# Where the matmul operands begin in SBUF: shifted starts in the input and activation buffers of a hybrid attention layer

## The reference, cut to what matters

```
p   = rms_norm(x, g_pre) @ w_in                  # 1024 -> 5064 columns: queries, keys, values, indexer, gates
o_a = sliding-window attention;  o_b = indexer, top 256 keys, attention over them
x   = x + rms_norm((sigmoid(g_a) * o_a + sigmoid(g_b) * o_b) @ w_o, g_post_mix)
hid = square(relu(rms_norm(x, g_pre_mlp) @ w_up))            # 1024 -> 4096
y   = x + rms_norm(hid @ w_down, g_post_mlp)                 # 4096 -> 1024
```

## Time and profile before

| | |
|---|---|
| median of 3 runs | 1902.87 us (1902.35 to 1903.76) |
| the profiled execution: its time | 1903.1 us |
| its span of instructions | 1901.3 us |
| TensorE matmul busy | 1879.1 us, 99% |
| TensorE weight load busy | 1778.6 us, 94% |
| VectorE, ScalarE, GpSimd busy | 1136.7, 712.9, 611.2 us |

### The profile page before, as it was taken

How to read it: one execution, slowest core, us unless ns; L and a number is a source line. 1 busy time by engine, 2 the same in 40 slices (tenths; PEclk the granted TensorE clock), 3 DMA queues, 4 the chain that set the end, 5 groups by cost and what they waited for, 6 DMA issues and landing times.

```text
span 1901.3 us, 32833 instructions
## 1 busy us (share of the span) xinstructions
PE 1879.1 (99%) x11892; PEld 1778.6 (94%) x11892; DVE 1136.7 (60%) x2694; ACT 712.9 (37%) x1424; POOL 611.2 (32%) x493
## 2 busy tenths in 40 slices
PE   9999999999999999999999999999999999999997
PEld 8899999877778999999998889999999999999996
DVE  5259999999765667676664553333333333333336
ACT  5345554233345556555673442222222222222222
POOL 4225554134344334444341022222222222222223
PEclk9999999999999999999999999999999999999999
DMA  6433333233556444444323331111111111111114
GB/s 205 116 84 85 99 95 94 83 107 91 124 134 144 102 102 102 102 102 91 68 69 126 114 126 45 45 44 44 44 44 44 44 44 44 44 44 44 44 44 144
DMA packets 180398, 160.26 MB, mean 84 GB/s; under 512 B 101472, under 2 KB 148432, under 8 KB 180288
## 3 DMA queue, kind: packets, MB, share of 16 engines
q1 hardware_dynamic: 164816, 139.72, 25.9%
q10 hardware_dynamic: 15472, 19.09, 4.4%
HBM read 120.63 MB, written 39.27 MB: 84 GB/s over the span
## 4 chain that ended last, share of the span: by engine, by line
PE 93%; DVE 2%; DMA 0%; issue 0%; SPq 0%; ACT 0%; DVEq 0%
PE ps L1084 23%; PE ps L1906 20%; PE ps L2472 19%; PE ps L1806 11%; PE ps L1782 6%; PE ps L1764 5%; PE ps L2153 5%; PE ps L1056 2%; PE ps L2134 0%; PE ps L2000 0%; DVE y L2416 0%; PE ps L1111 0%; DVE probs L1692 0%; DMA m_in<-merged_scr 0%; DVE total L2396 0%
## 5 line engine op out<-in xcount | busy, mean ns | idle before, releaser
L2472 PE MATMUL ps<-hid_hi,weights 128*128 128x362 f32 (+1 forms) x1536 | 380.3, 327 | 0.0
L1906 PE MATMUL ps<-x2T_hi,weights 128*128 128x362 f32 (+1 forms) x1536 | 378.0, 326 | 0.0
L1906 PEld LDWEIGHTS ps<-x2T_hi,weights 128*128 128x128 f32 x1536 | 272.1, 188 | 0.1
L2396 DVE TENSOR_TENSOR total<-total,ps 128x362 f32<-128x362 f32 (+1 forms) x360 | 189.2, 532 | 138.5 <-PE ps L2472 138.5
L2472 PEld LDWEIGHTS ps<-hid_hi,weights 128*128 128x128 f32 x1536 | 270.4, 188 | 0.0
L1906 PE MATMUL ps<-x2T_lo,weights 128*128 128x362 f32 (+1 forms) x768 | 251.4, 327 | 0.0
L2472 PE MATMUL ps<-hid_lo,weights 128*128 128x362 f32 (+1 forms) x768 | 250.2, 326 | 0.0
L1084 PE MATMUL ps<-xT_hi,w 128*128 128x362 f32 (+1 forms) x960 | 246.1, 330 | 1.6 <-PEq L181 1.6
L2381 DVE TENSOR_TENSOR hidden<-hidden 128x362 f32<-128x362 f32 (+1 forms) x96 | 51.5, 537 | 293.5 <-ACT hidden L2356 293.5
L1893 POOL TENSOR_TENSOR weights<-down_raw,weights 128x512 fp32r<-128x512 f32 x64 | 83.8, 1312 | 380.6 <-ACT weights L1887 380.6
L1035 DVE MATCH_REPLACE8 score<-top,score 128x1024 f32<-128x1024 f32 (+5 forms) x208 | 199.3, 967 | 0.0
(11 more groups left out here) (200 smaller groups left out, 3332.8 us busy)
## 6 DMA issues: line engine op xcount, KB each, us to landing
q_raw<-q_scr SPq DMA_DIRECT2D x80, 256.0 KB, 5.0
w_raw<-in_w_in ACTq DMA_DIRECT2D x64, 256.0 KB, 3.0
up_raw<-in_w_up SPq DMA_DIRECT2D x64, 256.0 KB, 2.8
down_raw<-in_w_down SPq DMA_DIRECT2D x64, 256.0 KB, 2.6
gates<-gate_scr SPq DMA_DIRECT2D x34, 256.0 KB, 4.5
x_in<-in_x_prompt SPq DMA_DIRECT2D x16, 512.0 KB, 5.2
gate_scr<-stage SPq DMA_DIRECT2D x32, 256.0 KB, 3.1
q_scr<-stage SPq DMA_DIRECT2D x40, 181.0 KB, 3.1
```

What stands on the lines that cost most here:

```text
L1906: last = pe.matmul(ps[:, bank, 0:n], a[:, k, fs], b, start=(k == 0 and i == 0), stop=(k == KT - 1 and i == 2))
L2396: dve.tensor_tensor(out, out, more, ALU.add).then_inc(added, 1)
L2472: more = pe.matmul(ps[:, falling_bank(g, final), 0:n], a[:, f, cols], h, start=(f == 0 and i == 0), stop=(f == FT - 1 and i == 2))
```

## The change

The three pairs of activation buffers become flat and 32 fp32 elements (128 bytes) longer, and the data begin some elements into them: 10 elements (40 bytes) for `xT` and `x2T`, 2 elements (8 bytes) for `hid`. The helper `moved` returns the same three-dimensional view as before, shifted. The sums by which later tensors are placed grow with it: 256 bytes for each pair. No instruction, wait or transfer is added or removed.

```diff
+def moved(tensor, first, rows, n):
+    return tensor[:, first:first + rows * n].rearrange("p (k n) -> p k n", n=n)
+
+LINE, X_FIRST, HIDDEN_FIRST = 32, 10, 2
-X_BYTES = 2 * 4 * KT * N_TOK
+X_BYTES = 2 * 4 * (KT * N_TOK + LINE)
...
-    out = place(nc, *first, FOOT, ("xT_hi", [P, KT, N_TOK], F32R), ("xT_lo", [P, KT, N_TOK], F32R), ("w", [P, 4, KT, 512], F32R),
+    out = place(nc, *first, FOOT, ("xT_hi", [P, KT * N_TOK + LINE], F32R), ("xT_lo", [P, KT * N_TOK + LINE], F32R), ("w", [P, 4, KT, 512], F32R),
...
-    return out | {"w_lo": out["w"][:, 0:4:2], "w_hi": out["w"][:, 1:4:2]}
+    return out | {"w_lo": out["w"][:, 0:4:2], "w_hi": out["w"][:, 1:4:2]} | \
+        {n: moved(out[n], X_FIRST, KT, N_TOK) for n in ("xT_hi", "xT_lo")}
...
-AFTER_TOTAL = UP_RAW_END + 4 * (2 * D + 2 * 364 + 2 * FT * N_QUERY + KT * N_QUERY)
+AFTER_TOTAL = UP_RAW_END + 4 * (2 * D + 2 * 364 + 2 * (FT * N_QUERY + LINE) + KT * N_QUERY)
...
-        hid_hi = sb("hid_hi", [P, FT, N_QUERY], F32R)
-        hid_lo = sb("hid_lo", [P, FT, N_QUERY], F32R)
+        hid_hi = moved(sb("hid_hi", [P, FT * N_QUERY + LINE], F32R), HIDDEN_FIRST, FT, N_QUERY)
+        hid_lo = moved(sb("hid_lo", [P, FT * N_QUERY + LINE], F32R), HIDDEN_FIRST, FT, N_QUERY)
...
-            x2T = [ctx.enter_context(nc.sbuf_tensor(n, [P, KT, N_QUERY], F32R)) for n in ("x2T_hi", "x2T_lo")]
+            x2T = [moved(ctx.enter_context(nc.sbuf_tensor(n, [P, KT * N_QUERY + LINE], F32R)), X_FIRST, KT, N_QUERY)
+                   for n in ("x2T_hi", "x2T_lo")]
```

## The result

| | before | after |
|---|---|---|
| median of 4 runs each, side by side | 1902.93 us | 1915.76 us (1914.85 to 1918.24) |
| span of the profiled execution | 1901.3 us | 1913.1 us |

The ratio is 1.0071 (95% interval 1.0055 to 1.0086): slower by some 13 us, outside the range of 1884 to 1911, on the other side of no change, and on the figure of rival (c), 1916. The first reading is the page of the kernel after: the span, each engine's busy time, and of the costliest groups the two that stream the hi parts in the MLP and VectorE's costliest (busy time, mean ns of one | idle time before them).

A forecast was written before the change was run, and what follows sets the result against it. TensorE's matmuls, busy 1879.1 of 1901.3 us, were taken as the bound. MLP -6.3 and projection -0.5 sum to -6.8 us against 1903.1, giving 1896 us, range 1884 to 1911.

The forecast's parts named there:

- rival (c): MLP blocks: cheapness hangs on place within 256 bytes relative to the weights; all six near 166.7 ns, +12.7 us, 1916; chance 0.25.
- Up product, block 1: from 24 to 23 pieces, 164.6 to 160.2: MLP up product, middle token block: one 64-byte piece fewer makes each matmul 4.4 ns cheaper, -3.4 us.
- I count the pieces of 64 bytes that an operand touches: MLP streamed operands of 362 columns: touching 23 pieces costs 160.2 and 160.4 ns, touching 24 costs 164.6.
- Down block 2, -3.2: MLP down product, last token block: from 24 to 23 pieces, 164.6 to 160.4 ns each, -3.2 us.
- Up block 2, 0: MLP up product, last token block: 23 pieces before and after, so no change.
- Down block 1, 0: MLP down product, middle token block: 23 pieces before and after, so no change.
- Projection, -0.5: Projection's streamed blocks: block 1 goes from 24 to 23 pieces, 1.0 ns each, -0.5 us; the other two 0.
- Gates, 0: Gate matmuls, activations stationary: starts shift 40 bytes; between a 4.0 us gain and an equal loss, taken as 0.
- bounds of the unknown terms: Whole kernel: all streamed blocks at 160.2 ns gives -31 us together, all at 167.1 ns gives +20 us.
- Rival (a): MLP: starting at byte 0 is dear in itself, so block 2 costs 166.7 ns in both products; +3.0 us, 1906; chance 0.22.
- Rival (b): MLP blocks 0: 364 columns from byte 40 fall to about 160 ns, a further -10.3 us, 1886; chance 0.15.
- Rival (d): MLP: nothing moves, because something other than addresses, perhaps PSUM banks, sets the distances; 1903 us; chance 0.05.

The follow-up runs named there:

- scan by 64 bytes: Against the original kernel with longer, unshifted buffers: x2T and hid begin 64 bytes further on; 1907.7 us in one run.
- shift without skew: The changed kernel with each buffer 256 bytes longer than originally, so lo keeps hi's place within 256 bytes instead of lying 128 off; 1909.4 us, ratio 1.0039.
- experiment 8: Against the original with longer, unshifted buffers: hid 128 bytes further, first with x2T 256 further too (1903.5 us), then hid alone (1904.5 us).
- best kernel: Against the kernel before: all MLP activation blocks at 224, 144, 56 within 256, hi and lo alike, projection lo 128 bytes off hi; 1894.5 us, ratio 0.9957.

## Why the prediction was wrong

What bounds the kernel was read rightly: the loss is made of distances between TensorE's matmuls, in the MLP, and nothing else moved. **The step that failed** is "Up product, block 1: from 24 to 23 pieces, 164.6 to 160.2", the term called the surest, and with it the reading under it, "I count the pieces of 64 bytes that an operand touches". Four rows of 362 columns were sorted by a rule that was chosen after looking at them; four rows can be sorted by many. The scan by 64 bytes leaves every start within 64 bytes in place and moves up block 2 from 160.2 to 164.8 and down block 1 from 160.4 to 163.3.

- Up block 1, -3.4 us: measured +0.10 us a chunk, +1.6. The test that the prediction set itself, 7.69 us for this block, gave 8.00, and it had said what that means: 64 bytes are the wrong measure. Down block 2, -3.2: measured +0.8. Without the skew it did fall to 160.4, but by its place, 192 of 256: up block 2 has the same start within 64 bytes and stands at 166.7 there.
- Up block 2, 0: measured +0.42 us a chunk, +6.7 us, the largest of all. It lost the place at which it was cheap (the shift without skew has it at 166.7), and the skew added 2.3 ns. Down block 1, 0: +2.9 us. The shift alone took it from 160.4 to 169.0, the skew gave 4.8 ns back. Down block 0, 0: +1.3, and up block 0, +0.3: +0.2. Without the skew these two stand at 166.7 and 163.3.
- Projection, -0.5: blocks 1 and 2 by the rows -1.5 and 0 ns, some -0.7 us. That term was right in sign and size, and over the whole stretch the projection's streamed blocks take 0.3 us less. Gates, 0: 231.3 to 232.9 ns, some +1.4 us over 864 matmuls (+0.9 over the whole stretch), within its bounds of 4.
- The bounds of the unknown terms, -31 and +20 us around no change, held. The ceiling for one block, 167.1 ns, didn't: two of them reached 169.
- Rival (a) failed as it was stated, for both blocks 2. Block 2 from start 0 within 64 is indeed not cheap at place 128, but at place 192 it is (160.4 in the shift without skew). Of its evidence this stands: 362 columns from byte 0 are dear (166.7).
- Rival (b), blocks 0 at about 160 from byte 40, failed: from place 40 the block costs 163.3 without the skew and 166.9 with it, and 163.3 is the least that 364 columns cost at any place tried.
- Rival (d) failed with the first result.
- Rival (c) was right, in its price (12.7 us against 13.4) and its mechanism: place within 256 bytes, relative to the weights. The two kernels with moved weights show the relation, in one run each. It isn't the whole mechanism: experiment 8 adds a dependence on what ran before, which no rival had. Its second half, the skew, is shown by the kernels with and without it: 1909.4 to 1915.8. Its assumption that all six would stand at 166.7 was coarse: they run from 164.2 to 169.0, and that they come to the same sum is partly luck.

The evidence for (c) stood in the prediction's own rows: the projection's block 2 has the start within 64 bytes that was to be cheap and costs 165.7. It was used there to hold down a small term, and not to doubt the rule that made the large ones. A row against a rule drawn from four was a reason to give (c) no less than the forecast.

The Trainium skill's Part 2 of TensorE: Matmul & The Clock Gate, weighed in the prediction, says that loading the next weights takes no read bandwidth from the running matmul. This trace of alternating loads and matmuls doesn't agree that the two go on unhindered by each other: with only the weights moved, up block 2 went from 160.2 to 166.7 ns and down block 2 from 164.6 to 160.2, and with both operands moved alike they stood where they had been. Whether it is read bandwidth that is short isn't shown.

**What stays open.** The mechanism. Distances that hang on the difference of two addresses within 256 bytes, and on what ran before, fit two reads that fall in or out of step with each other, but no run shows the memory itself. Which places are cheap can't be foretold: 16, 56, 88, 144 and 192 have shown about 160 ns with 362 columns, and 88 and 144 have shown 166.5 or more too. How long the work before is remembered was not tried; in the cases under 8 the other distance lasts for the whole block of 48 matmuls.

## What to carry to other kernels

Where every matmul has its own weight load and TensorE is the bound, measure the distance between starts by block: if equal shapes differ, operand starts are a free tuning parameter (here 0.4% down and 0.7% up). Vary them by measurement, all products together, since one product's places change another's distances; keep hi and lo at one place within 256 bytes unless a run shows better. And a rule read from as many rows as it sorts is a guess: look for the row that it gets wrong before giving it the largest terms.

## What was unexpected of the hardware

- The distance between matmuls with the same 362 columns, shapes and clock went from 160.0 to 169.0 ns with nothing changed but addresses: 9 ns, 6%.
- Moving both operands by 128 bytes changes none of the MLP's six distances by more than 0.2 ns; moving one changes single blocks by up to 6.5 ns. It is so in the output product too, with 512 columns: 226.7 ns before, 233.3 with its lo weights, which stream in one of three matmuls, 128 bytes on.
- The same places can stand at 160.2 or at 166.7 ns for a whole block; what ran before differs between the two, and in the best kernel that holds within one execution.
- 364 columns never went under 163.3 ns at the places tried, while 362 went to 160.0. Why two columns make that much isn't shown.
